# Expert rows added to the residual in DRAM by indirect accumulating transfers, instead of stored and gathered

## What is computed

```python
logits = (xt @ w_router + b_router)
top_vals, top_idx = lax.top_k(logits, TOP_K)          # 4 of 32 experts
weights = jax.nn.softmax(top_vals, axis=-1)
...
def expert_block(args):
    xblk, e = args
    gu = xblk @ w_gu[e] + b_gu[e]                     # 1024 -> 2048
    gate, up = jnp.split(gu, 2, axis=-1)
    gate = jnp.minimum(gate, SWIGLU_LIMIT)
    up = jnp.clip(up, -SWIGLU_LIMIT, SWIGLU_LIMIT)
    act = (up + 1.0) * gate * jax.nn.sigmoid(SWIGLU_ALPHA * gate)
    return act @ w_down[e] + b_down[e]                # 1024 -> 1024
...
y = jnp.zeros((n_tok + 1, D_MODEL)).at[buf_tok].add(yb * buf_w[:, None])
h = h + g2 * y
return rmsnorm(h, final_norm_w)                       # and the second block starts from it
```

## Time and profile before

| | |
|---|---|
| median of 3 runs | 2183.75 us (2177.44 to 2184.8) |
| the profiled execution | 2187.41 us, its span 2185.6 us |
| mean granted clock of PE | 0.948 of full speed |
| PE, DVE, ACT, POOL busy | 91%, 43%, 13%, 12% of the span |
| DMA queue 1 (issued by SP) | 537.38 MB, 62.1% of the 16 DMA engines' span |

### The profile page before, as it was taken

One profiled execution on the slowest core, in us unless ns is written; L12 is line 12 of the kernel. 1 busy time (PEld: TensorE's weight loads), 2 busy tenths in 40 slices (PEclk: granted clock), 3 DMA queues, 4 the chain that ended last, 5 costly groups with the idle time before them and its releaser, 6 DMA issues. The chain is left out here.

```text
span 2185.6 us, 42671 instructions
## 1 busy us (share of the span) xinstructions
PE 1979.0 (91%) x17735; PEld 1052.4 (48%) x17735; DVE 934.4 (43%) x1792; ACT 275.1 (13%) x545; POOL 251.7 (12%) x285
## 2 busy tenths in 40 slices
PE   5889986999889998989898984799998999999998
PEld 3445553444234444434343432444776558885443
DVE  2552443333233332323232334465646465546564
ACT  2221230000000000000000001343233120000000
POOL 1930001111001110101010113000220000000000
PEclk9999997999899999999999997799998899999999
DMA  9476758999999999999999998510101402323441
GB/s 361 160 192 193 271 198 321 368 415 421 423 422 422 421 422 421 422 422 422 422 422 423 421 422 295 202 38 0 40 26 40 164 1 77 108 85 135 182 171 60
DMA packets 137555, 570.09 MB, mean 261 GB/s; under 512 B 19082, under 2 KB 32542, under 8 KB 88162
## 3 DMA queue, kind: packets, MB, share of 16 engines
q1 hardware_dynamic: 114416, 537.38, 62.1%
q0 software_dynamic: 6640, 19.30, 2.4%
q10 hardware_dynamic: 16354, 11.21, 1.6%
HBM read 550.91 MB, written 25.31 MB: 264 GB/s over the span
## 5 line engine op out<-in xcount | busy, mean ns | idle before, releaser
L1411 PE MATMUL ps<-W,x_modulated 128*32 128x512 f32 x2640 | 325.8, 616 | 41.2 <-DMA W<-in_w_gu 30.6
L1556 DVE TENSOR_SCALAR gate<-ps 128x256 f32<-128x256 f32 x77 | 32.7, 424 | 552.1 <-PE ps L1415 552.1
L1411 PEld LDWEIGHTS ps<-W,x_modulated 128*32 128x32 f32 x2640 | 90.9, 111 | 228.6 <-issue 156.1
L1411 PE MATMUL ps<-W_high,x_modulated 128*32 128x512 f32 x1376 | 174.0, 612 | 16.4 <-DMA W_high<-in_w_gu 13.8
L1427 PE MATMUL ps<-W,hidden_turned 128*32 128x256 f32 x2736 | 163.8, 383 | 0.0
L1500 ACT ACTIVATE sig<-gate 128x256 f32<-128x256 f32 x81 | 33.8, 417 | 947.4 <-DVE gate L1556 901.0
L1923 PE MATMUL ps<-turned_rows,W 128*128 128x512 f32 x336 | 148.0, 599 | 2.5 <-PEq L131 2.2
L1427 PEld LDWEIGHTS ps<-W,hidden_turned 128*32 128x32 f32 x2736 | 101.9, 111 | 61.8 <-issue 19.4
L1381 POOL COPY rows_idx<-slot_rows 128x1 int32 (+1 forms) x83 | 23.0, 277 | 831.9 <-DVE x_turned L1541 825.6
L2972 PE MATMUL ps<-turned_rows,W 128*128 128x256 f32 x512 | 116.4, 380 | 2.3 <-PE ps L2972 1.9
L3129 PE MATMUL ps<-W,mix_room 128*128 128x512 f32 x256 | 115.2, 593 | 1.7 <-PEq L2278 1.5
(11 more groups left out here) (583 smaller groups left out, 2710.6 us busy)
## 6 DMA issues: line engine op xcount, KB each, us to landing
W<-in_w_gu SPq DMA_DIRECT2D x139, 1024.0 KB
W<-in_w_down SPq DMA_DIRECT2D x71, 1024.0 KB
W_high<-in_w_gu SPq DMA_DIRECT2D x69, 1024.0 KB
W_high<-in_w_down SPq DMA_DIRECT2D x35, 1024.0 KB
W<-in_mlp_w SPq DMA_DIRECT2D x32, 1024.0 KB, 5.9
W<-in_w_ada SPq DMA_DIRECT2D x12, 2048.0 KB, 9.2
turned_rows<-in_w_gu SPq DMA_DIRECT2D x24, 1024.0 KB
h<-in_w_gu SPq DMA_DIRECT2D x24, 1024.0 KB
```

Of the source, the lines that this page charges most:

```text
L1411: last = pe.matmul(gu_out(j), xs[:, kk, :], quarter(ex.view(n), j), start=kk == 0, stop=False)
L1556: dve.tensor_scalar(gate[:], gu_bank[:, 0:256], SWIGLU_LIMIT, None, ALU.min).then_inc(gated, 1)
```

## The change

Nothing is stored in `moe_y` any more, and that tensor is gone. POOL adds each sub-block's rows straight to the residual `moe_h` in DRAM, with an indirect transfer that accumulates (`compute_op=ALU.add`). The rows' route weights are multiplied in by DVE's `weighted`, from a second table `slot_w`. Two transfers could name the same residual row, so POOL waits for each before it issues the next (`y_added`). Slots without a token point at 128 extra rows past the residual, which are filled with zeros. So 2 transfers of 128 KB take the place of the 16 zero fills. Both tables come from wide one-hots on DVE, and PE now makes each of them by 64 matmuls with 32 stationary columns. `Combine` reloads the four tiles of `h` with plain transfers. ACT has no transfers left, and its copies to `turned_rows` and three of its four `keep` go to DVE and POOL.

```diff
-            spare = 2 * E_ * SUB
-            fills = (MAX_SUBS * SUB - spare) // P
-            for i in range(fills):
-                sp.dma_start(k.y[spare + i * P:spare + (i + 1) * P, :], a["const_zero"].to_broadcast([P, D])).then_inc(zero_out, 16)
...
+            for rows_of in (moe.xn, moe.h):
+                sp.dma_start(rows_of[NO_TOKEN:NO_TOKEN + P, :], a["const_zero"].to_broadcast([P, D // 4])).then_inc(zero_out, 16)
...
-            pool.wait_ge(destd, 1)
-            for j in range(HI_POOL):
-                pool.tensor_scalar(hi_of(j), iota[:], dhif[:, j:j + 1], None, ALU.is_equal).then_inc(hid_p, 1)
...
+            pe.wait_ge(lod, 1)
             for j in range(TT * TOPK):
-                pe.wait_ge(lod, j + 1)
-                if j < HI_POOL:
-                    pe.wait_ge(hid_p, j + 1)
-                else:
-                    pe.wait_ge(hid_v, j - HI_POOL + 1)
-                pe.matmul(ps[2][:, 0:MAX_SUBS], lo_of(j), hi_of(j), start=j == 0, stop=j == TT * TOPK - 1).then_inc(slot_mm, 1)
+                pe.wait_ge(hid, j // 8 + 1 if j < 12 else 3)
+                for q in range(4):
+                    last = pe.matmul(ps[2][SUB * q:SUB * (q + 1), 0:MAX_SUBS], lo_rows[:, j, :], hi_of(j), start=j == 0, stop=j == TT * TOPK - 1)
+            last.then_inc(slot_mm, 1)
+            pe.wait_ge(lod, 2)
+            for j in range(TT * TOPK):
+                for q in range(4):
+                    last = pe.matmul(ps[3][SUB * q:SUB * (q + 1), 0:MAX_SUBS], lo_w[:, j, :], hi_of(j), start=j == 0, stop=j == TT * TOPK - 1)
+            last.then_inc(slot_w, 1)
...
-            for j in range(TT * TOPK):
-                if j >= 8:
-                    dve.wait_ge(slot_mm, j - 7)
-                dve.tensor_scalar(lo_of(j).rearrange("p (c l) -> p c l", c=4), iota[:, 0:SUB].rearrange("p (o l) -> p o l", o=1).to_broadcast([P, 4, SUB]),
-                                  dlof[:, j:j + 1], tok4[:, j // TOPK:j // TOPK + 1], ALU.is_equal, ALU.mult).then_inc(lod, 1)
-                if j >= HI_POOL:
-                    if j >= 12:
-                        dve.wait_ge(slot_mm, j - 11)
-                    dve.tensor_scalar(hi_of(j), iota[:], dhif[:, j:j + 1], None, ALU.is_equal).then_inc(hid_v, 1)
...
+            link(dve.tensor_tensor(lo_w, iota[:, 0:SUB].rearrange("p (o l) -> p o l", o=1).to_broadcast([P, TT * TOPK, SUB]), spread(dlof[:], SUB), ALU.is_equal))
+            dve.tensor_tensor(lo_rows, lo_w, spread(row_off[:], SUB), ALU.mult).then_inc(lod, 1)
+            for lo, hi, hot_rows in ((0, 8, hi_hot[:, 0:8, :]), (8, 12, hi_hot[:, 8:12, :]), (12, 16, hi_late[:])):
+                dve.tensor_tensor(hot_rows, iota[:].rearrange("p (o n) -> p o n", o=1).to_broadcast([P, hi - lo, MAX_SUBS]), spread(dhif[:, lo:hi], MAX_SUBS), ALU.is_equal).then_inc(hid, 1)
...
-            dve.wait_ge(slot_mm, TT * TOPK)
-            dve.tensor_scalar(moe.idx4[:], ps[2][:, 0:MAX_SUBS], moe.quarter[:, 0:1], None, ALU.add).then_inc(idx_ready, 1)
...
-            link(dve.tensor_tensor(moe.weights[:], gaps[:], ssum[:].rearrange("p (i o) -> p i o", o=1).to_broadcast([P, TT, TOPK]), ALU.mult))
+            link(dve.tensor_tensor(route_w[:], gaps[:], ssum[:].rearrange("p (i o) -> p i o", o=1).to_broadcast([P, TT, TOPK]), ALU.mult))
+            dve.tensor_tensor(lo_w, lo_w, spread(route_w[:].rearrange("p i q -> p (i q)"), SUB), ALU.mult).then_inc(lod, 1)
+            dve.wait_ge(slot_mm, 1)
+            dve.tensor_scalar(moe.idx4[:, 0:MAX_SUBS], ps[2][:, 0:MAX_SUBS], moe.no_row[:, 0:1], None, ALU.add).then_inc(idx_ready, 1)
+            dve.wait_ge(slot_w, 1)
+            dve.tensor_copy(moe.slot_w[:, 0:MAX_SUBS], ps[3][:, 0:MAX_SUBS]).then_inc(slot_w_ready, 1)
+            dve.wait_ge(slot_w_ready, 1)
...
-                if e == E_ - 1:
-                    for p in (MOE_SLOTS - 2, MOE_SLOTS - 1):
-                        last = max(q for q in range(E_ * CHUNKS) if q % MOE_SLOTS == p)
-                        sp.wait_ge(ex.read[last % CHUNKS], subs)
-                    sp.dma_start(k.h[:], m.h.rearrange("(i p) n -> p i n", p=P)).then_inc(h_in, 16)
...
-            with sp.Fori(first, end, 2) as i:
-                u = sp.snap(i)
-                sp.wait_ge(y_ready, u + 3)
-                for j in range(4):
-                    sp.dma_start(m.y[bass.ds(u * SUB + SUB, SUB), j * 256:(j + 1) * 256], yb_2[SUB * j:SUB * (j + 1), :]).then_inc(y_out, 16)
+            sp.wait_ge(y_out, end + 1)
...
+            def next_gather(u):
                 pool.wait_ge(x_in, u * 16)
 
                 pool.wait_ge(x_turn, u)
                 gather(u)
-            pool.wait_ge(y_out, end * 64 + 64)
+
+            def scatter(u, held=yb):
+
+                pool.tensor_copy(to_idx[:], m.idx4[:, bass.ds(u, 1)]).then_inc(to_set, 1)
+                pool.wait_ge(to_set, u + 1)
+                pool.wait_ge(y_ready, u + 2)
+                pool.sem_inc(scatters, 1)
+                pool.indirect_dma_start(m.h, bass.IndirectOffsetOnAxis(ap=to_idx[:, 0:1], axis=0), held[:] if held is yb else held, None, compute_op=ALU.add).then_inc(y_added, 16)
+                pool.wait_ge(y_added, u * 16 + 16)
+                pool.sem_inc(y_out, 1)
...
+            pool.sem_inc(y_out, 1)
+            gather(0)
...
+            next_gather(1)
+            with pool.Fori(0, start, 2) as i:
+                u = pool.snap(i)
+                next_gather(u + 2)
+                next_gather(u + 3)
+                scatter(u)
+                scatter(u + 1, yb_2)
+            next_gather(start + 2)
+            with pool.Fori(start, last_but_one) as i:
+                u = pool.snap(i)
+                next_gather(u + 3)
+                scatter(u)
+            next_gather(first + 1)
+            scatter(last_but_one)
+            scatter(pool.value_load(m.table[0:1, E_ + 1:E_ + 2], min_val=2 * LAST - 1, max_val=MAX_SUBS - 3))
+            with pool.Fori(first, end, 2) as i:
+                u = pool.snap(i)
+                next_gather(u + 2)
+                scatter(u)
+                scatter(u + 1, yb_2)
+                next_gather(u + 3)
+            pool.wait_ge(x_in, end * 16 + 32)
             pool.sem_inc(gathers, 1)
             combine.gpsimd(pool)
...
-            def rows(u, held=yb):
-
-                act.wait_ge(y_ready, u + 2)
-                for j in range(4):
-                    act.dma_start(m.y[bass.ds(u * SUB, SUB), j * 256:(j + 1) * 256], held[SUB * j:SUB * (j + 1), :]).then_inc(y_out, 16)
...
-            act.wait_ge(y_out, end * 64 + 64)
-            act.sem_inc(rows_out, 1)
+            with act.Fori(0, end) as i:
+                sigmoid(act.snap(i))
             combine.scalar(act)
...
+            def weighted(u, rows, bank):
+                dve.scalar_tensor_tensor(out=rows, in0=bank[:, 0:256], scalar=m.slot_w[:, bass.ds(u, 1)], in1=g4[:], op0=ALU.mult, op1=ALU.mult).then_inc(y_ready, 1)
...
-                dve.wait_ge(y_out, u * 64 + 64)
+                dve.wait_ge(y_out, u + 1)
                 dve.wait_ge(down_done, u + 1)
-                dve.tensor_tensor(yb[:], down_bank[:, 0:256], g4[:], ALU.mult).then_inc(y_ready, 1)
+                weighted(u, yb[:], down_bank)
...
-        w = self.w
-        sp.wait_ge(self.added, TT * TOPK - 2)
+        k, m, w = self.k, self.m, self.w
+        for i in range(TT):
+            sp.dma_start(k.h[:, i, :], m.h[i * 4 * P:(i + 1) * 4 * P, :].rearrange("(t q) c -> t (q c)", q=4)).then_inc(self.h_in[i], 16)
         for c in (3, 2, 4, 5):
             n = w.first["in2"] + c
...
     def gpsimd(self, pool):
-        m, NB = self.m, self.NB
-        for j in range(TT * TOPK):
-            if j >= NB:
```

More of the change, by code:

```diff
@@ L388, in _ @@
             ex.load(sp, 21)
[L389 removed]
+            sp.wait_ge(zero_out, 32)
         @block.scalar
@@ L1384, in gather @@
                 pool.indirect_dma_start(xg[:], None, m.xn, bass.IndirectOffsetOnAxis(ap=rows_idx[:, 0:1], axis=0)).then_inc(x_in, 16)
-            gather(0)
-            end = total(pool)
-            with pool.Fori(1, end + 2) as i:
-                u = pool.snap(i)
+            def next_gather(u):
                 pool.wait_ge(x_in, u * 16)
@@ L1636, in __init__ @@
         self.k, self.w, self.m, self.hT = k, w, m, hT
-        NB = self.NB
-        self.rows = k.high[:, 0:NB * D].rearrange("p (b n) -> p b n", b=NB)
-        self.gained = k.high[:, NB * D:(NB + TT) * D].rearrange("p (i n) -> p i n", i=TT)
+        self.gained = k.high[:, 6 * D:(6 + TT) * D].rearrange("p (i n) -> p i n", i=TT)
         self.fw, self.junk = k.gate_rows[:, 0, :], k.high[:, 11 * D:12 * D]
@@ L1652, in sync, with keep, gained @@
             sp.dma_start(w.tile(n), w.jobs[n][0]).then_inc(w.loaded[w.slot[n]], 16)
+    def keep(self, i):
+        return self.k.h[:, i, :], self.gained[:, i, :], self.root[:, i, 0:1]
     def gpsimd(self, pool):
-        m, NB = self.m, self.NB
-        for j in range(TT * TOPK):
-            if j >= NB:
-                pool.wait_ge(self.added, j - NB + 1)
```

(45 more changed lines are left out.)

131 lines of the change are left out of this document (56 added, 75 removed).

## The result

The changed kernel took 2218.56 us, the median of 4 runs (2211.51 to 2221.67), against 2183.11 for the kernel before (4 runs, 2177.44 to 2184.8). The ratio is 1.0157, 95% interval 1.0141 to 1.0174: **slower by 35 us**. The profiled execution took 2218.36 us, with a span of 2216.5. I had said 2188, within 2160 to 2235.

What follows compares the result with a forecast made beforehand. The prediction took DMA transfers, mostly weights, to bound the expert stage. Its terms, 18 + 0 - 18 + 3.5 + 0 = +4 us on the median of 2183.75, gave 2188 us, range 2160 to 2235.

Steps and rivals of the forecast that it cites:

- A: The forecast case: the scatter's two reads are paid and POOL's turn is covered; 2175 to 2218 us, chance 0.42.
- rival C: Clearly slower: the scatter's landing sets the pace, one POOL turn per sub-block; 2205 to 2290 us, chance 0.25.
- L: Time from the start of a scatter's issue to its landing, taken as 7.5 us; cover gone at 9.4.
- What bounds the kernel now: Expert stage: transfers are full, DMA share 1.01, mean sub-block 12.23 us; DMA time added or saved counts in full.
- Part 1: Expert stage: a scatter takes 0.65 us of DMA time, +0.23 us per sub-block, +18 us; bounds -6 and +33.
- Part 2: POOL's turn of gather, scatter and landing wait: 10.6 us, covered by the weights' pace of 12.5, cost 0.
- Part 3: Combine, last result to PE's second-block start: additions go, two landings in series come; -18 us, bounds -22 and -8.
- Part 4: Routing: wide one-hots and PE's 64 groups of four matmuls delay the first gather; +3.5 us, bounds +1 and +10.
- Part 5: Removed zero fills, 8.4 MB: they were covered by PE's projections, so 0 us.
- Rival B: Faster: the scatter's second read is hidden because writes set the engines' pace; 2163 us, range 2155 to 2175, chance 0.33.

Runs made afterwards that it cites:

- experiment 1: The changed kernel with a scatter that writes its rows without adding them: 2166.7 us, ratio 0.9923 to the kernel before.
- experiment 3: The changed kernel with both edits, the next gather issued before the scatter lands and a scatter that doesn't add: 2159.61 us, ratio 0.9895.
- experiment 6: The kernel of experiment 2 with a scatter that adds only 128 of each partition's 256 columns: 2169.15 us, ratio 0.9936 to the kernel before.
- experiment 7: The kernel of experiment 2 with rows of empty slots dropped by both gather and scatter: 2187.68 us, ratio 1.0015 to the kernel before.
- experiment 8: The kernel of experiment 2 with rows of empty slots dropped by the scatter alone: 2187.27 us, ratio 1.0022 to the kernel before.
- experiment 2: The changed kernel with POOL's next gather issued before the scatter has landed, same transfers and sums: 2191.49 us, ratio 1.0034 to the kernel before.
- experiment 4: The changed kernel with some 1.0 us more work on POOL ahead of each gather, no transfer added: 2257.39 us, ratio 1.0329 to the kernel before.

## Why the prediction was right in its sign and range, and wrong in its case

The range held and slower was the likeliest sign, but the case I took, A, isn't what happened; **rival C is, in its mild form** (its 2219 us stood at L = 9.8; measured 2218.6 at some 9.5). That its number was met so closely is luck. Its 31 us for the turn stood at L = 9.8, and at 9.5 its formula gives 8. The wait cost 27, the sum's DMA time was 14 us more than the forecast under it held, and smaller errors gave some 10 back. By steps:

- **What bounds the kernel now**: right. Taking DMA time out showed in the time in experiments 1, 3 and 6, though not in 7 and 8. The share alone doesn't tell the bound: it is 1.01 in the changed kernel, whose weights often wait for places, and 1.02 in experiment 2, which is 27 us faster. And the mean of 12.23 us, right as a mean, is the pace of hardly any sub-block.
- **Part 1, the scatter's DMA time**: the right mechanism, mis-sized. The term was "0.34 + 0.31 = 0.65 us", so +0.23 a sub-block and +18 us. Measured: 9.4% of 917 us over 74 sub-blocks in experiment 2 is 1.16 us for gather and scatter, so 0.82 for the scatter, +0.40 and 79 x 0.40 = +32 us. The 2x2 table gives 31.9, just under my upper bound (+33). Without the sum a scatter is 5.6% of 917 over 77, less 0.34: 0.33 us, a gather's price, which was my lower bound. By the rule of the Trainium skill ("Collectives: The Full Stack", why ReduceScatter is half of AllGather) a sum moves at half the rate of a copy; the direction agrees with the trace, and the factor here was 2.5 (0.82 against 0.33).
- **Part 2, the turn of POOL**: this step failed. It said "I cost the turn at 0", and the wait cost 27.1 us: 21.5 in the stage and 5 in the combine. Two things in it were wrong. L was not 7.5 us but 9.5 (the fixed work was 3.08 against my 3.10). And the turn was compared with the mean pace. "At L = 9.5 it costs 0.1 x 77 = 8 us" is by that comparison, and with the sum's real price (12.63 us a sub-block) it gives nothing at all. The pace of before is 10.65 to 11.34 us in 63 of 74 sub-blocks, and a turn of 12.6 stretches those; by my reading under experiment 3, the 22 places for weights made up for only part of it. The four stores' 9.5 us were the right number but no evidence: they were taken as the stream ended (DMA share 0.61 from 1336 to 1341 us, 0.05 from 1341 to 1345), over four issues. The same holds for the gather's 5.4, which I called "beside the weights". For a plain scatter 7.5 was good: in experiment 1, L was some 7.4 where POOL waited for it, and the wait cost 0.7 us in the stage (7.1 in all). Two more claims of this part were wrong. "What is late first is not the gather": it was the gather as much as DVE's result, since POOL issues it behind the landing (DVE waited for its rows 61 times). And "every further microsecond 77 us": one microsecond cost 39, for the most part because the landing got shorter as the turns got longer.
- **Part 3, the combine**: right: 35.6 us against my 38, so -20 against -18. The last gather that I counted (1.1 + 5.4 us, then three DVE operations) is there: `h` had landed at 1397.82, and DVE came to it at 1403.9, behind `place_x`. With the early gather it went out beside the last scatter, and the combine took 30.6.
- **Part 4, the routing**: right in the main: the copy of the second table was done at 343.35 (343.8 predicted; less 340.11 that is 3.7, not 3.5), and PE's first matmul came 2.1 us later. PE's clock stood at 0.50 from 333.1 to 338 us, longer than the 3.5 us that I took.
- **Part 5, the zero fills**: right: PE unchanged, 0 us.
- **Rival B** falls with the sum's price, but its number was a good one for a free sum: 2163 us, where experiments 1 and 3 gave 2166.7 and 2159.6.

My forecast of 2188 was by chance what the changed kernel would do without the wait (2191.5): there, part 1's missing 14 us are mostly made good by a combine of 30.6 us instead of 38 and by a second block that took 791.5 us against 795.5.

## What to carry to other kernels

A transfer that sums into DRAM is dearer than a write twice over: in DMA time (0.82 against 0.33 us here) and in landing time (8.7 against 6.2), and the second reaches whatever is queued behind the wait for it. If such a wait must be there, put the next independent issue ahead of it; that one reordering gave back 27 us of 59. And compare the length of such a chain with the pace of the sub-blocks that run fastest (10.66 us here), not with the mean (12.23): where the pace alternates, a turn at the mean takes away the catching up, and here the wait cost 21.5 us of stage though the turn was at the mean. Take the landing from a row that ran beside the same stream, and look up the DMA share of that very stretch.

## What the runs showed of the hardware that I had not expected

- The landing of a scatter isn't a constant: 9.5 us beside the full weight stream, 3.9 after the stream's end (1390.49 to SP's reload at 1394.34), 4.3 in a pause of it (172 GB/s in 1323 to 1327 us of experiment 4).
- The scatter's issue on POOL took 1.60 us with the sum and 1.01 without, and a gather 1.00. The sum also tripled its packets. A gather has 48 (3648 over 76). Experiment 2's 14256 are 75 gathers and 74 scatters of 144, and experiment 1's 7296 are 152 transfers of 48, gathers and scatters alike.
- ACT loaded its function table in each turn of the new loop (122.38 us busy in 144 rows, 31.27 in 75 before); it lies behind the sigmoid, and nobody waited for it:

```profile
805.16 0.42 ACT L1526 ACTIVATE sig<-gate 128x256 f32<-128x256 f32 x1 [10.47 <-DVE gate L1556]
805.63 1.28 ACT L1526 ACT_TABLE_LOAD   x1
```
